# Two GpSimd subtractions in the handover, and residual sums cut in halves at the end, in a retention and convolution decoder layer

## The reference, cut to what matters

```python
def layer(h, pos, ret_state, conv_buf, ...):
    xn = rms_norm(h, n_mix_pre)
    proj = xn @ w_in                       # q, k, v, g, a, b
    ret_out  = retention(q, k, v) normed * silu(g)
    conv_out = conformer_conv(a, b, ...)
    mix = jnp.concatenate([ret_out, conv_out], axis=-1) @ w_out
    h = h + rms_norm(mix, n_mix_post)
    xf = rms_norm(h, n_ffn_pre)
    gate, up = jnp.split(xf @ w_ffn_in, [D_FF], axis=-1)
    h = h + rms_norm((jax.nn.silu(gate) * up) @ w_ffn_out, n_ffn_post)
```

## Time and profile before

| | |
|---|---|
| median of 3 runs | 1178.29 us (1177.98 to 1179.56) |
| the profiled execution's own time | 1177.31 us |
| its span in the trace | 1175.4 us |
| TensorE busy | 1148.9 us, 98% |
| VectorE busy | 802.2 us, 68% |
| GpSimd busy | 610.2 us, 52% |
| ScalarE busy | 444.3 us, 38% |
| mean granted TensorE clock | 0.993 |

### The profile page before, as it was taken

One profiled execution on the slowest core, in us unless ns is written; L12 is line 12 of the kernel. 1 busy time (PEld: TensorE's weight loads), 2 busy tenths in 40 slices (PEclk: granted clock), 3 DMA queues, 4 the chain that ended last, 5 costly groups with the idle time before them and its releaser, 6 DMA issues.

```text
span 1175.4 us, 22876 instructions
## 1 busy us (share of the span) xinstructions
PE 1148.9 (98%) x8646; PEld 1129.1 (96%) x8646; DVE 802.2 (68%) x1242; ACT 444.3 (38%) x798; POOL 610.2 (52%) x455
## 2 busy tenths in 40 slices
PE   8999999999999999799999999999999999999997
PEld 7999999999999986699999999999999999999997
DVE  6368999954555247987685858584848585867646
ACT  6454454232334336642424233333333233333313
POOL 2066788304122357566565656474747473737316
PEclk9999999999989999899999999999999999999999
DMA  9311111111154223212121211212121212121134
GB/s 292 118 36 55 37 54 55 37 48 55 41 149 117 90 90 127 73 37 73 37 72 36 65 42 44 64 36 71 36 71 36 71 36 71 36 71 36 55 143 165
DMA packets 102360, 84.53 MB, mean 72 GB/s; under 512 B 2722, under 2 KB 89378, under 8 KB 102298
## 3 DMA queue, kind: packets, MB, share of 16 engines
q1 hardware_dynamic: 102258, 83.68, 23.2%
q10 hardware_dynamic: 48, 0.10, 0.0%
HBM read 72.86 MB, written 11.38 MB: 72 GB/s over the span
## 4 chain that ended last, share of the span: by engine, by line
PE 85%; DVE 5%; POOL 5%; issue 3%; DMA 2%; ACT 1%; DVEq 0%; SPq 0%; POOLq 0%; ACTq 0%
PE ps L409 26%; PE ps L411 26%; PE ps L410 26%; DVE w_ring L1601 1%; DMA f_raw<-in_w_ffn_in 1%; POOL o_last L825 1%; POOL h_ring L783 1%; PE ps L1965 1%; PE ps L1895 1%; PE ps L1914 1%; POOL st L616 1%; PE ps L2019 1%; PE ps L2018 1%; DMA x_st<-in_x_prompt 1%; DVE x_lo L1595 0%
## 5 line engine op out<-in xcount | busy, mean ns | idle before, releaser
L1737 DVE TENSOR_TENSOR ffn_acc<-ps,ffn_acc 128x516 f32<-128x516 f32 x264 | 183.6, 696 | 8.0 <-PE ps L411 2.6
L409 PE MATMUL ps<-xn_hi,w_hi 128*128 128x350 f32 (+2 forms) x576 | 187.2, 325 | 0.9 <-DVE xn_lo L1296 0.9
L411 PE MATMUL ps<-xn_lo,w_hi 128*128 128x350 f32 (+2 forms) x576 | 185.2, 322 | 0.0
L410 PE MATMUL ps<-xn_hi,w_lo 128*128 128x350 f32 (+2 forms) x576 | 184.9, 321 | 0.0
L409 PE MATMUL ps<-x_hi,w_ring 128*128 128x256 f32 x616 | 175.5, 285 | 5.8 <-DVE e_s L1615 3.8
L409 PE MATMUL ps<-x,w_ring 128*128 128x260 f32 x616 | 175.4, 285 | 1.6 <-issue 1.2
L410 PE MATMUL ps<-x,w_ring 128*128 128x260 f32 x616 | 175.3, 285 | 0.0
L411 PE MATMUL ps<-x,w_ring 128*128 128x260 f32 x616 | 175.0, 284 | 0.0
L410 PE MATMUL ps<-x_hi,w_ring 128*128 128x256 f32 x616 | 174.1, 283 | 0.0
L411 PE MATMUL ps<-x_lo,w_ring 128*128 128x256 f32 x616 | 174.1, 283 | 0.0
L409 PE MATMUL ps<-act_hi,w_ring 128*128 128x258 f32 x560 | 158.2, 283 | 0.1
(11 more groups left out here) (257 smaller groups left out, 2672.4 us busy)
## 6 DMA issues: line engine op xcount, KB each, us to landing
f_raw<-in_w_ffn_in SPq DMA_DIRECT2D x42, 512.0 KB, 3.9
raw<-in_w_in SPq DMA_DIRECT2D x24, 512.0 KB, 3.9
f_raw<-in_w_ffn_out SPq DMA_DIRECT2D x22, 512.0 KB, 4.1
x_st<-in_x_prompt SPq DMA_DIRECT2D x8, 512.0 KB, 8.6
raw<-in_w_out SPq DMA_DIRECT2D x8, 512.0 KB, 6.6
h_ring<-in_x_prompt SPq DMA_DIRECT2D x8, 512.0 KB, 4.1
h_scratch<-h_ring SPq DMA_DIRECT2D x8, 512.0 KB, 3.1
h_fin<-h_scratch SPq DMA_DIRECT2D x8, 512.0 KB
```

The lines of the kernel that those rows point to most:

```text
L409: nc.tensor.matmul(out, hi, mhi, start=first, stop=False, skip_group_check=resumes)
L410: nc.tensor.matmul(out, lo, mhi, start=False, stop=False, skip_group_check=resumes)
L411: return nc.tensor.matmul(out, hi, mlo, start=False, stop=last, skip_group_check=resumes)
L1737: v.tensor_tensor(a, tile_banks(i), a, ALU.add).then_inc(s_acc, 1)
```

## The change

In the handover, the second low part of the sums (block rows 20 to 27) of the tiles 5 and 7 goes from VectorE to GpSimd. The new function `x_sums_lo(t)` on GpSimd stands after the residual addition at t = 8 (for tile 5), and after `x_sums_14(8)` at t = 10 (for tile 7). TensorE's counts follow. At the end, `out_add` of the positions 4 and 5 is cut into two halves of 512 columns, with the root steps between them, the residual addition of the sample tile (o = 6) on VectorE goes from the last place to the place just after its scaling, and the stores follow in another order.

```diff
+SPLIT_SUMS = (5, 7)
...
-            for i in range(2):
-                sp.wait_ge(s_yd, 2 + i)
-                store(LAST_ORDER[8], slice(i * 512, (i + 1) * 512))
+            sp.wait_ge(s_yd, 3)
+            store(LAST_ORDER[8], slice(0, 512))
             sp.wait_ge(s_y, 6)
             store(LAST_ORDER[5], slice(0, D))
             sp.wait_ge(s_yd, 4)
-            store(LAST_ORDER[6], slice(0, D))
+            store(LAST_ORDER[8], slice(512, D))
...
+            def x_sums_lo(t):
+
+                xh, xl, xs = x_block(t)
+                pool.wait_ge(s_xs14, t // 2 * 2 + 2)
+                pool.wait_ge(s_shi, t // 2 * 2 + 2)
+                g.tensor_tensor(xl[:, 20:28], xs[:, 20:28], xh[:, 20:28].bitcast(F32), ALU.subtract).then_inc(s_clo, 1)
...
                 if t >= 2 and (t % 2 or t == 10):
                     x_sums_14(t - 2)
+                if t in (8, 10):
+                    x_sums_lo({8: 5, 10: 7}[t])
...
             out_power(0)
-            for o in range(5):
+            for o in range(4):
                 out_power(o + 1)
                 out_add(o)
+            out_power(5)
+            out_add(4, 0, 512)
             out_power(6)
+            out_add(4, 512, D)
             out_power(7)
+            out_add(5, 0, 512)
             out_power(8)
-            out_add(5)
+            out_add(5, 512, D)
...
-                for i, q in enumerate((12, 20)):
+                for i, q in enumerate((12,) if t in SPLIT_SUMS else (12, 20)):
                     dve.wait_ge(s_shi, t // 2 * 2 + i + 1)
                     v.tensor_tensor(xl[:, q:q + 8], xs[:, q:q + 8], xh[:, q:q + 8].bitcast(F32),
                                     ALU.subtract).then_inc(s_slo, 1)
...
             out_var(6)
             out_var(7)
             out_scale(6)
+            t = LAST_ORDER[6]
+            dve.wait_ge(s_fsc, 7)
+            v.tensor_tensor(o_last[0:NS, t, :], o_last[0:NS, t, :], h_fin[t][0:NS, :], ALU.add).then_inc(s_yd, 1)
             out_var(8)
             out_finish(7, slice(0, D), 1)
             out_finish(8, slice(0, 512), 2)
             out_finish(8, slice(512, D), 2)
...
                         elif p == 1:
-                            pe.wait_ge(s_slo, 2 * pairs - 1)
+                            pe.wait_ge(s_slo, 2 * pairs - 1 - len(SPLIT_SUMS) * ss)
                         elif p == 4:
-                            pe.wait_ge(s_slo, 2 * pairs)
+                            pe.wait_ge(s_slo, 2 * pairs - len(SPLIT_SUMS) * ss)
+                            if ss:
+                                pe.wait_ge(s_clo, len(MIX_TILES) + 1 + len(SPLIT_SUMS))
```

More of the change, by code:

```diff
@@ L592, in _ @@
             sp.wait_ge(s_yd, 1)
+            store(LAST_ORDER[6], slice(0, D))
+            sp.wait_ge(s_yd, 2)
             store(LAST_ORDER[7], slice(0, D))
-            for i in range(2):
-                sp.wait_ge(s_yd, 2 + i)
-                store(LAST_ORDER[8], slice(i * 512, (i + 1) * 512))
+            sp.wait_ge(s_yd, 3)
+            store(LAST_ORDER[8], slice(0, 512))
             sp.wait_ge(s_y, 6)
@@ L818, in out_power, with out_add @@
                 power(st[0:n, q + 2:q + 3], st[0:n, q + 1:q + 2], s_var, 9 + o + 1, s_rstd)
-            def out_add(o):
+            def out_add(o, c0=0, c1=D):
                 t = LAST_ORDER[o]
@@ L824, in out_add @@
                 pool.wait_ge(s_fsc, o + 1)
-                g.tensor_tensor(o_last[0:n, t, :], o_last[0:n, t, :], h_fin[t][0:n, :], ALU.add).then_inc(s_y, 1)
+                ins = g.tensor_tensor(o_last[0:n, t, c0:c1], o_last[0:n, t, c0:c1], h_fin[t][0:n, c0:c1], ALU.add)
+                if c1 == D:
+                    ins.then_inc(s_y, 1)
             pool.wait_ge(s_gpre, 32)
@@ L1774, in _ @@
             out_finish(8, slice(512, D), 2)
-            t = LAST_ORDER[6]
-            dve.wait_ge(s_fsc, 7)
-            v.tensor_tensor(o_last[0:NS, t, :], o_last[0:NS, t, :], h_fin[t][0:NS, :], ALU.add).then_inc(s_yd, 1)
         @block.tensor
```

## The result

The changed kernel takes 1181.65 us, the median of 8 runs (1180.42 to 1184.38), and the kernel before 1178.38 (8 runs, 1176.39 to 1179.56). The ratio is 1.0029 with a 95% interval from 1.002 to 1.0038, so the change costs 3.4 us (2.4 to 4.5). The execution that was profiled took 1180.42 us, with a span of 1178.6 us (1175.4 before) and a mean granted clock of 0.991.

The account below looks back on a forecast made before the run. VectorE was taken to bound the handover and the last stores the end; 0 up to k = 0, +2.1 at k = 1 and +0.6 at the end gave +2.7 us on 1178.29, so 1181.0 us, range 1177.5 to 1183.5.

Parts of the forecast that it names:

- the sample tile's store: In the last stream of stores: 32 KB going ahead of o = 7, reckoned at 0.1 us.
- What holds VectorE: VectorE and GpSimd instructions with two SBUF operands wait for each other's whole length, taking turns; PSUM-operand work keeps its length.
- Tile 5: Handover, k = -4: VectorE's next subtraction waits for GpSimd's moved 2.3 us, so TensorE's product starts 1.1 us later.
- Tile 7: Handover: the removed subtraction pays back tile 5's delay, 0 at k = 0; GpSimd's moved one makes k = 1 2.1 us later.
- Restart: TensorE's restart behind the handover, at 504.69 us before: 2.1 us later, as all VectorE work up to there shifts.
- The end: After the last matmul: the continuous stream of last stores starts later and ends 0.6 us later; bounds -0.4 to +1.5.
- the 0.7 of the sum: At the end: out_finish(7) on VectorE starts 0.7 us later, behind the sample tile's addition.
- The far bound of +1.5: At the end: GpSimd's half goes ahead of the sample tile's addition, 1.2 us more on VectorE; +1.5 us instead of +0.6.
- Rival (a): TensorE's idle gap before k = 1 lowers its clock, costing 1.7 us more, for 1182.7 us; chance 0.20.
- Rival (b): Handover: the moved work does not hold VectorE, k = 1 comes 2.3 us earlier, for 1176.6 or 1173.9 us; chance 0.08.
- Rival (c): Handover's delay is partly hidden or the end gains by its earlier root: +1 us in all, 1179.3 us; chance 0.22.
- The base: The sum was added to the earlier kernel's runs' median, 1178.29 us, 0.98 above its profiled execution of 1177.31.

Follow-up runs that it names:

- e_drop: e_hand with the two moved low-part subtractions done on no engine, ScalarE copying 8 block rows of the sums instead; 1176.59 us against 1179.11 before the change.
- e_hand: The kernel before with only the handover's half of the change (both low parts on GpSimd), end as before; 1180.41 us against 1179.11.
- e_memset: e_drop with a GpSimd fill of 128x1024 in an unused buffer where the moved subtractions stood; 1178.03 us against 1179.11 before the change.
- e_tail: The kernel before with only the end's half of the change, handover as before; 1179.83 us against 1179.11.
- x_tailorder: e_tail with GpSimd's first half for o = 5 put behind the root of o = 8; 1178.77 us against 1179.15 before the change.
- e_samp: The kernel before with only the sample tile's earlier addition on VectorE and the change's store order; 1179.28 us against 1177.61.
- e_t7: e_hand with only tile 7's second low part moved to GpSimd, tile 5's staying on VectorE; 1180.44 us against 1177.61 before the change.
- the eight experiments of the first two sets: Eight kernels: each half of the change alone, the moved work left out or replaced by fills, and single parts of the halves; 1176.59 to 1180.44 us.
- x_t5late: The kernel before with only tile 5's second low part moved to GpSimd, behind the root of tile 8; 1180.3 us against 1179.15.

## Why the prediction was right, point by point

The predicted 1181.0 us is 0.65 under the median, and the sum of +2.7 us stands against 3.4 measured. It was right for the reason that it gave, with one term at its far bound, the sample tile's store sized too small, and one detail of the order wrong.

**What holds VectorE.** Shown by `e_drop` beside `e_hand` (-2.04 against +2.01 us; `e_hand` has the two subtractions on GpSimd, `e_drop` has two copies on ScalarE in their place) and by `e_memset`, where GpSimd is busy at the same places. For work with a PSUM operand, which keeps its length, the prediction's example is weak: L1709 at 1.27 us has only roots of 0.54 beside it. `out_finish` shows it better: the 1024 columns that begin at 1167.97 in the earlier trace rows take 1.26 us, half of them beside L825.

**Tile 5, predicted +1.1 us.** Measured +1.17, and L702 takes 2.35 us where 2.3 was reckoned from the earlier trace rows. But the order is not the one predicted. VectorE's low part had waited since 480.42 and was to go next; GpSimd's L702 went first, at 481.55, and VectorE's instruction stands for 4.57 us instead of the next L1618 for 2.9. The delay is the same, because the same two pieces of work stand one after the other whichever is first; so the right total was no proof of the turns.

**Tile 7, predicted 0 at k = 0 and +2.1 at k = 1.** Measured +0.02 and +2.17. Here the order was as predicted: GpSimd's L702 begins at 497.12, ahead of VectorE's small low parts, and ends at 499.93; VectorE's first ends at 499.98. TensorE's wait of 2.38 us was put at about 2.5.

**Restart, predicted +2.1.** Measured +2.01.

**The end, predicted +0.6: the step that failed.** Measured +1.43 (1.44 in `e_tail`). Two terms were wrong. The first is the order. The prediction said that VectorE adds the sample tile behind the root of o = 7, ends at 1168.6, and that GpSimd's half of o = 5 "had to wait for the sample tile". It was the other way round: the half began at 1169.34, 0.02 us ahead of the end of the root, and VectorE's addition, begun at 1169.02, waited for both. Counted from the start of the last matmul (1168.8 before, 1170.6 now), `out_finish(7)` stood at -0.8 us (1167.97) and stands at +1.1 (1171.67), 1.9 later: the 0.7 of the sum and 1.2 more, which is GpSimd's half. The far bound of +1.5 named this very case. `x_tailorder` takes the half out of the way, and the end comes back by all of its 1.44 us.

The second is the sample tile's store. The sum gave it 0.1 us of the stream, by its 32 KB. In the traces' list of DMA packets it is eight packets of 4 KB that take about 0.25 to 0.6 us each, where those of the large stores mostly take 0.16 or 0.08. In `x_tailorder`, `e_samp` and the change they stand apart, 0.80 us behind the end of VectorE's addition, which is how they are known. Behind the large stores, as before, they end 0.46 us after them (5.89 against 5.43 us after the last matmul); ahead of them they are over before the large ones begin. The last three large stores take 4.1 us in either place. So the end moves by the later start of the large stores, less 0.46:

```
kernel        large stores begin    last end  later start - 0.46    measured end
before               1.31           5.43 (with the sample tile's 5.89)
x_tailorder          1.78           5.88     0.47 - 0.46 = 0.01        0.00
e_samp               2.54           6.65     1.23 - 0.46 = 0.77        0.77
the change           3.23           7.31     1.92 - 0.46 = 1.46        1.43
```

With the order as predicted, the term would have been about 0, not 0.6, as `x_tailorder` has it; the +0.6 lay nearer to the measured 1.43 by an error the other way.

**Rival (a), the clock falls in the new gap** (0.20). It didn't in the profiled execution nor in `e_hand`, with gaps of 2.38 and 2.37 us, and did in `e_t7` with 2.36. Its price was 1.7 us; `e_t7` shows 1.14. Whether it happens in some of the changed kernel's other runs, one trace can't say.

**Rival (b), the moved work doesn't hold VectorE** (0.08). Its own sum, 2.3 us earlier in the handover, is what `e_drop` has (-2.30 at k = 1), so the pieces were sized rightly and the mechanism excluded it. Its hope for more from the clock fell too: with the gap before k = -4 down to 2.70 us in `e_drop`, the first matmul behind it still takes 0.55 us and the clock is 0.50.

The timeline of TensorE in `e_drop` at k = -4:

```profile
484.41 0.55 PE L410 MATMUL ps<-x_hi,w_ring 128*128 128x256 f32 x1 [2.70 <-DVE e_s L1628]
```

**Rival (c), less than reckoned** (0.22): no part of the handover's 2 us was hidden, and the end gained nothing by its earlier root.

**The base.** The sum was put on the median of before. "Early" and "groups" move by up to 3 us from trace to trace and cancel in part here (+1.02 and -1.24); that a difference of two single spans (3.2) came near that of the runs (3.4) is luck, and only the matmul starts counted from a common place made the terms readable.

## What to carry to other kernels

The sizes here are this kernel's. Before work with two SBUF operands goes from VectorE to GpSimd, see what VectorE has next: where that is dense in instructions with two SBUF operands, the move takes 1.2 us off VectorE and puts GpSimd's own 2.0 to 2.3 us on it, while a fill, which has no SBUF input, cost nothing (`e_memset`). Reckon such an edit as GpSimd's duration on VectorE's line, unless the rows show a gap, or PSUM work, as long as the whole instruction; being released by the same event as VectorE's next instruction is the worst place. When a small GpSimd step that others wait for stands between long ones, put it first and the long one behind VectorE's instruction (`x_tailorder`). Don't size a small store by its bytes: at the very end this one of 32 KB cost 0.46 us. And split the effect of an edit by stage from the starts of the same matmuls, since the spans alone differ by more than the edit.

## What the runs showed of the hardware that was not expected

**Who goes next.** In the traces of before, of the change and of the eight experiments of the first two sets, 202 times a VectorE instruction with two SBUF operands had stood waiting for over 0.05 us when a GpSimd instruction ended and another of GpSimd's that reads SBUF began by that end. In 197 of them VectorE went next, as in the earlier trace rows, and in five it didn't. The five come at two places, in each kernel that has this order there: behind L792 at tile 5 (in the change, `e_hand` and `e_t5`), and behind the root of o = 7 at the end (in the change and `e_tail`), where GpSimd's second instruction went ahead and VectorE stood for 4.57 and 2.65 us. The Trainium skill, page "SBUF — State Buffer", section "Who interferes with whom", says that the order of issue decides who blocks; these rows differ, since VectorE's instruction is the earlier one in them by 1.1 us (480.42 against 481.55), and the measurement decides. At both places an instruction on 8 partitions takes part (L792 at the one, L1790 at the other), but that is a guess, and no run tried it. Against it speaks a third place, ahead of the handover: before, VectorE's L1453 begins at 389.49, 0.04 us ahead of the end of a GpSimd instruction, and GpSimd's L719 at 389.50. L719 goes first in its 1.28 us, and L1453 stands for 2.37, with nothing on 8 partitions beside it. What decides stays open.

**The scaling takes part too.** The instruction with a scalar and two tensors (`h_scale`) waits for GpSimd like the subtraction (3.39 us for 1.27 in `x_t5late`), and GpSimd's residual addition beside it (L783) takes 3.35 us, where the shortest of the nine takes 2.39.

**The clock after nearly the same gap.** After 2.36 to 2.38 us of idle TensorE the granted clock stayed at 1.00 in two kernels and fell to 0.50 in a third, and in `x_t5late` it fell behind one of 1.33 us. It also falls with no idle time at all. The stretches around 350 us, before:

```profile
348.00:352.00 4.00, 4.00 (x29) 4.00 (x28) 3.71 (x4) 2.07 (x4) 1.44 (x1) 0.73 0.82 209
```

And in the changed kernel:

```profile
348.00:352.00 4.00, 4.00 (x21) 4.00 (x20) 3.28 (x4) 1.53 (x2) 0.80 (x1) 0.50 0.57 161
```

TensorE is busy all the time in both, and in the four microseconds that are shown the one makes 29 matmuls and the other 21. The edits are 130 us further on, so this is chance. It is most of "early" here: the changed kernel is 0.6 us ahead of the one before up to 340 us, and 1.0 behind it from 355 on. By "early" alone, from -0.8 to +3.2 us, the spans of these kernels differ for nothing.
